# Neighbourhood attention: the turning of the weights is multiplied by a diagonal of reciprocal sums

## The reference

```python
s_loc = jnp.einsum("bqhd,biqjhd->bhqij", q_r, k_win).astype(jnp.float32) * scale
s_loc = s_loc + bias.astype(jnp.float32)
s_ctx = jnp.einsum("bqhd,bchd->bhqc", q_r, kc).astype(jnp.float32) * scale
s = jnp.concatenate([s_loc.reshape(B, H, GRID_W, n_loc), s_ctx], axis=-1)
p = jax.nn.softmax(s, axis=-1).astype(v.dtype)
p_loc = p[..., :n_loc].reshape(B, H, GRID_W, kh, NA_KW)
return (jnp.einsum("bhqij,biqjhd->bqhd", p_loc, v_win)
        + jnp.einsum("bhqc,bchd->bqhd", p[..., n_loc:], vc))
```

## Time and profile before

| what | us |
|---|---|
| median of three executions (lowest, highest) | 3058.83 (3057.3, 3061.13) |
| the profiled execution | 3055.73 |
| its span, first to last instruction | 3053.9 |
| TensorE busy with matmuls in it | 2975.5 |
| VectorE busy | 2074.0 |
| ScalarE busy | 1412.6 |
| GpSimd busy | 241.1 |
| all turning matmuls of the attention (line 2296), within 1978 to 2104 us | 9.66 |

### The profile page before, as it was taken

How to read it: one execution, slowest core, us unless ns; L and a number is a source line. 1 busy time by engine, 2 the same in 40 slices (tenths; PEclk the granted TensorE clock), 3 DMA queues, 4 the chain that set the end, 5 groups by cost and what they waited for, 6 DMA issues and landing times.

```text
span 3053.9 us, 52430 instructions
## 1 busy us (share of the span) xinstructions
PE 2975.5 (97%) x21994; PEld 2632.0 (86%) x21994; DVE 2074.0 (68%) x2869; ACT 1412.6 (46%) x1977; POOL 241.1 (8%) x201
## 2 busy tenths in 40 slices
PE   8999999999999999999999999999989999999998
PEld 7899988887888888888888899888878888888887
DVE  6486864645656787888888985555677666666666
ACT  5343542534444563544445454444336445444453
POOL 1100321110100200000000310010010000000002
PEclk9999999999999999999999999999999999999999
DMA  7555566766645669888888877755345565665664
GB/s 250 166 167 156 158 222 206 225 196 227 209 138 159 214 198 280 274 277 277 273 279 277 271 234 225 221 151 170 109 131 162 183 187 178 202 187 184 180 186 132
DMA packets 527580, 619.94 MB, mean 203 GB/s; under 512 B 19450, under 2 KB 443541, under 8 KB 525984
## 3 DMA queue, kind: packets, MB, share of 16 engines
q1 hardware_dynamic: 518672, 586.31, 62.2%
q0 software_dynamic: 3344, 23.78, 2.2%
q10 hardware_dynamic: 5328, 6.49, 0.6%
HBM read 608.12 MB, written 8.39 MB: 202 GB/s over the span
## 4 chain that ended last, share of the span: by engine, by line
PE 90%; DVE 5%; issue 3%; ACT 1%; DMA 0%; POOL 0%; ACTq 0%; POOLq 0%; DVEq 0%; SPq 0%
PE psum L605 37%; PE psum L606 19%; PE psum L574 6%; PE psum L576 6%; PE psum L577 6%; PE psum L639 2%; PE psum L641 2%; PE psum L642 2%; DVE wlo L531 1%; PE psum L1851 1%; PE psum L706 1%; DVE cacc L1118 1%; PE psum L2563 1%; PE psum L2082 0%; PE psum L2304 0%
## 5 line engine op out<-in xcount | busy, mean ns | idle before, releaser
L524 ACT ACTIVATE whi<-wraw 128x1024 fp32r<-128x1024 f32 (+1 forms) x948 | 978.6, 1034 | 1001.2 <-PE psum L606 692.7
L531 DVE TENSOR_TENSOR wlo<-wraw,whi 128x1024 fp32r<-128x1024 f32 (+1 forms) x948 | 1151.2, 1230 | 244.6 <-ACT whi L524 244.1
L605 PE MATMUL psum<-g,whi 128*128 128x512 f32 x2816 | 996.1, 396 | 11.0 <-DVE g L2603 4.1
L605 PE MATMUL psum<-h,whi 128*128 128x512 f32 x2240 | 790.7, 395 | 2.3 <-DVE wlo L531 1.3
L606 PE MATMUL psum<-g,wlo 128*128 128x256 f32 x2816 | 787.0, 279 | 0.0
L605 PEld LDWEIGHTS psum<-g,whi 128*128 128x128 f32 x2816 | 529.0, 188 | 139.9 <-issue 8.4
L606 PE MATMUL psum<-h,wlo 128*128 128x256 f32 x2240 | 634.1, 283 | 0.0
L606 PEld LDWEIGHTS psum<-g,wlo 128*128 128x128 f32 x2816 | 529.2, 188 | 0.5
L605 PEld LDWEIGHTS psum<-h,whi 128*128 128x128 f32 x2240 | 421.4, 188 | 100.3 <-DVE wlo L531 1.6
L606 PEld LDWEIGHTS psum<-h,wlo 128*128 128x128 f32 x2240 | 421.9, 188 | 0.1
L574 PE MATMUL psum<-h,whi 128*128 128x256 f32 x1040 | 304.0, 292 | 22.0 <-DVE h L958 13.7
(11 more groups left out here) (488 smaller groups left out, 3191.3 us busy)
## 6 DMA issues: line engine op xcount, KB each, us to landing
wraw<-in_ffn_w SPq DMA_DIRECT2D x256, 512.0 KB, 4.9
wraw<-in_w_in SPq DMA_DIRECT2D x204, 512.0 KB, 3.7
wraw<-in_ada_w SPq DMA_DIRECT2D x192, 512.0 KB, 4.2
wraw<-in_ffn_w_up SPq DMA_DIRECT2D x160, 512.0 KB, 3.6
wraw<-in_w_out SPq DMA_DIRECT2D x64, 512.0 KB, 3.7
wraw<-in_ffn_w_down SPq DMA_DIRECT2D x64, 512.0 KB, 4.5
wraw<-in_xattn_wk SPq DMA_DIRECT2D x32, 512.0 KB, 4.6
wraw<-in_xattn_wv SPq DMA_DIRECT2D x32, 512.0 KB, 4.9
```

Of the source, the lines that this page charges most:

```text
L524: e.activation(high(i), raw(i), ACT.Copy).then_inc(*hi.up(i))
L531: e.tensor_tensor(low(i), raw(i), high(i).bitcast(F32), SUB).then_inc(*lo.up(i))
L605: e.matmul(both_of(g, j), w_hi[:, kk, s:s + 128], X[:, k, :], start=k == 0, stop=False, skip_group_check=True)
```

## The change

The reciprocal of each unit's sums is no longer multiplied into the 128x512 buffer. VectorE multiplies the 128x128 identity by it and writes the diagonal matrix to a new tile, `DG`, with two buffers. The turning takes this diagonal as its moving side, and is a plain matmul, `e.matmul`, in place of `e.transpose`. The result in bank 5 is the same: block transposed, each query's column scaled. For units from 2 on, VectorE waits before it writes `DG` until the turning of two units earlier has read the same buffer.

```diff
@@ -342,6 +342,7 @@
         TMX = new("tmx", [P, 4, T])
+        DG = new("dg", [P, 2, P])
@@ -2293,7 +2294,8 @@
                         for k in range(4):
-                            x = e.transpose(PSUM[:, 5, 128 * k:128 * k + 128], weights_of(u)[:, 128 * k:128 * k + 128], ident)
+                            x = e.matmul(PSUM[:, 5, 128 * k:128 * k + 128], weights_of(u)[:, 128 * k:128 * k + 128], DG[:, u % 2, :], start=True,
+                                         stop=True)
                         x.then_inc(*nat.p.up(("pt", u)))
@@ -2321,11 +2323,13 @@
         def na_share_v(e, u):
-            p, s = weights_of(u), SM6[:, u % 8, :]
+            s = SM6[:, u % 8, :]
             e.wait_ge(*nat.a.at("e", u))
             e.reciprocal(s[:, 3:4], s[:, 2:3]).then_inc(*nat.v.up())
             e.wait_ge(*nat.v.now())
-            e.tensor_scalar(p, p, s[:, 3:4], None, MUL).then_inc(*nat.v.up(("p", u)))
+            if u > 1:
+                e.wait_ge(*nat.p.at("pt", u - 2))
+            e.tensor_scalar(DG[:, u % 2, :], ident, s[:, 3:4], None, MUL).then_inc(*nat.v.up(("p", u)))
```

## The result

Nine executions of the changed kernel took 3061.9 to 3070.5 us, with a median of 3065.3; nine of the kernel before had a median of 3058.0. The ratio on record is 1.0027, with a 95% interval of 1.0019 to 1.0035; the quotient of the two medians is 1.0024. So the changed kernel is slower, by 7.3 us between the medians. The forecast was 7.6 us more and 3066.4.

The account below looks back on a forecast made before the run. TensorE was taken to bound the attention's stretch. 7.4 us for second passes plus 0.2 for idle starts, with VectorE's saving hidden, made 3058.8 + 7.6 = 3066.4 us; the forecast's own range was 3065 to 3068, 8 in 10 3062 to 3070.

Parts of the forecast that it names:

- What bounds the stretch: Attention, 1978 to 2104 us: TensorE, busy 122.3 of 126 us, sets the end; anything added to its stream moves it.
- The second pass: Turning on TensorE: a plain float32 matmul makes two passes per call, 0.46 us more a unit, 7.4 us in 16 units.
- The value of 0.112 taken from line 1281: Turning on TensorE: time of one float32 pass in us, read from line 1281's same-shaped matmuls; eight make 0.90 us.
- The small term: Three units whose turning begins on an idle TensorE after the copy: 3 x 0.07 = 0.2 us more.
- VectorE's saving: VectorE's 16 multiplications, 128x128 in place of 128x512: 3.2 us saved, none of it on the path.
- The cover of unit 0: Attention: unit 0's division ends 6.8 us before its turning releases the chain, the narrowest of the 16.
- The 288 ns worked out for the diagonal: VectorE: time taken for one 128x128 multiplication, in place of 486 ns for 128x512.
- The added wait: VectorE before writing `DG`: of 3.46 us between turning and reciprocal, 3.0 us are left, so the wait costs nothing.
- Nothing absorbs it: TensorE's waits keep their length and later work moves whole; wrong if what follows the stretch changes by over 3 us.
- A plain matmul at a transpose's cost: Rival at the 64 turning calls: eight passes fit into 0.44 us, nothing is added, 3055.6 to 3058.8 us; chance 6%.
- One at four transposes: Rival at the turning: a plain float32 matmul costs four transposes, 1.32 us more a unit, 21 us, 3080; chance 2%.
- The slow clock: Rival, later in the block: stretches at clock 0.50 may go, saving 4.4 us, sum 3.2 us, 3062.0; chance 14%.

Follow-up runs that it names:

- Experiment 5: Kernel before, with VectorE multiplying each unit's 128x512 buffer by one four times more ahead of the division: ratio 0.9997, 3057.4 us beside 3058.6.
- experiment 6: Changed kernel with one buffer for the diagonal, so VectorE waits for the turning of the unit before: ratio 1.0019, 3064.7 us beside 3058.6 for the kernel before.
- experiment 2: Kernel before, with each unit's four transposes issued twice: ratio 1.0024, 3065.6 us beside 3057.6.
- experiment 8: Changed kernel with turning, scores and product with the values all in the rounded format: ratio 0.9927, 3037.7 us beside 3058.6 for the kernel before.
- experiment 1: Kernel before, with the turning as a plain float32 matmul against the identity and the division left on the 128x512 buffer: ratio 1.0021, 3065.2 us beside 3057.6.
- experiment 3: Changed kernel with the turning as a transpose against the identity again; the diagonal is written but unread: ratio 0.9998, 3057.2 us beside 3057.6 for the kernel before.
- experiment 7: Changed kernel with each block turned by two matmuls with stationary sides of 64 columns: one execution at 3069.1 us.
- experiment 4: Changed kernel with the diagonal and the exponentials written in the rounded format: ratio 0.9996, 3056.4 us beside 3057.6 for the kernel before.

## Why the prediction was right

- *What bounds the stretch.* Right. Experiment 5 gives VectorE 30.1 us more and experiment 6 makes it stand for 54.7, and the end doesn't move; experiments 2 and 8 add and take passes of TensorE, and the end moves by +6.94 and -20.00 us, as the passes say.
- *The second pass, 16 x 0.46 = 7.4 us.* Right: 128 records, 0.89 us for eight, 7.40 us in the stretch, and 7.35 in experiment 1 with nothing else changed. The value of 0.112 taken from line 1281 holds (0.89 / 8 = 0.111); experiment 2 puts the passes' count at 6.94 of it.
- *The small term, 0.2 us for groups on an idle engine.* Too large. With the term the stretch should have grown by 7.6, and it grew by 7.40. The group that starts after the wait stands with 1.13 us in the chain where the transposes' had 0.63 (in the chain as in the earlier trace rows), 0.05 more than the 0.45 that other groups gained (0.89 against 0.44), so 0.15 us in three units, and by the chain's figures the other groups gained 0.01 less than the 0.46 taken. The term was mis-sized by line 1281, whose first step is 0.10 over the others. A turning group on an idle engine lasts 1.13 us in order of time and the others 1.05, so that the plain matmul loses 0.08 there and not 0.10.
- *VectorE's saving, 3.2 us, hidden.* Right in both: experiment 3 has 3.14 us less and no gain. The cover of unit 0, given as 6.8 us, is 6.6 by the start of its turning; that reading decides nothing. The 288 ns worked out for the diagonal were 287 in the median. In the changed kernel itself the saving was 1.2 us (71.42 to 70.24), since more of the short instructions met GpSimd (last section); it cost nothing, being hidden.
- *The added wait.* Right, with no wait in the trace. Only the 3.0 us left of 3.46 is wrong. The changed kernel still has the 3.46, from the end of unit 6's turning to unit 8's reciprocal:

```profile
2041.90 1.05 PE L2297 MATMUL psum<-dg,tmx 128*128 128x128 f32 x8
...
2046.41 0.15 DVE L2328 RECIPROCAL sm<-sm 128x1 f32<-128x1 f32 x1
```

The reciprocal waits for work that hangs on TensorE itself, so it moves when the turning gets longer. Experiment 6 shows that even a wait that stands costs nothing here. The reason given ahead of that run, two chunks' low halves in store, is read from the order of the programs; the run shows only that TensorE's waits stay at 2.3 and 1.4 us.
- *Nothing absorbs it.* Right: TensorE's waits stay at 3.7 us. What lies after the stretch was 2.08 us shorter in the profile, less than the 3 set as a bound, and the medians differ by 7.3.
- *The rivals.* A plain matmul at a transpose's cost is off by experiment 1. One at four transposes would have made it 21 us more. By experiments 1 and 2 the two differ by 132.94 - 132.53 = 0.41 us at an equal number of passes, so nearly all of the mode's gain at 128 columns is the halved count, 0.89 / 0.44 = 2.0. The rule behind that rival, in the table of terms of the Trainium skill's TensorE: Matmul & The Clock Gate, is that the transposing mode is 4x faster for FP32; this trace doesn't agree, with 2.0. The slow clock did move, as the other rival had it, and in part its way: in the profiled execution of the changed kernel nothing stands at 0.50 where the first stretch of the earlier trace rows would be, but one near 2300 us lasts 6.8 us in place of 3.4. No gain of 4.4 us came of it, and it differs from execution to execution.

## What to carry to other kernels

Count the passes of a matmul before moving work to it: where a float32 transpose becomes a float32 matmul, its records double, and where TensorE sets the end each of them is on the path, here 64 x 0.112 us. An engine's saving is worth what the stretch's last wait says, and a dose in the other direction (experiment 5, ten times the saving, spent) shows at once whether it is worth anything. Where executions scatter by several us, cut the span at the same two instructions in both traces: the 7.4 us stood out to 0.05 us in each profile, while the times needed nine runs and more to show them.

## What the runs showed of the hardware

*The slow clock comes and goes between executions.* Up to the first score matmul the profiled executions took 1977.0 (experiment 1) to 1984.7 us (experiment 2), with the same instructions in all (in experiment 8 some write another format). In the changed kernel the granted clock was 0.50, 1.2 GHz, in stretches where it was 1.00 before, and the reverse. After:

```profile
368.70:372.00 3.30, 3.30 (x18) 3.30 (x17) 3.30 (x8) 0.24 (x1) 0.37 (x1) 0.50 0.00 1
...
2217.20:2223.90 6.70, 6.70 (x34) 4.49 (x32) 4.94 (x5) 0.00 (x0) 1.27 (x1) 1.00 0.02 9
```

Before, the first of these stood at the full clock and the second, of the earlier trace rows, at 0.50:

```profile
368.70:372.00 3.30, 3.30 (x31) 3.30 (x30) 3.30 (x7) 0.63 (x1) 1.13 (x1) 1.00 0.16 57
```

TensorE gets 18 matmuls through the first in place of 31. Ahead of the attention this goes far to account for the differences. The times of the ten profiles broadly follow the time that each spent at 0.50, added up from the traces' granted clock:

| at 0.50 ahead of the attention, us | profiles | first score matmul at, us |
|---|---|---|
| 13.7 | before, experiments 1 and 5 | 1977.0 to 1978.7 |
| 17.1 | experiments 7 and 8 | 1979.2 and 1980.0 |
| 20.5 | after, experiments 3 and 6 | 1979.1 to 1981.0 |
| 23.9 | experiment 4 | 1984.2 |
| 27.3 | experiment 2 | 1984.7 |

The 6.8 us between before and after can cost 3.4 at most, since the clock is halved, and the measured difference is 1.88. Behind the attention the clock doesn't suffice. Leaving out the very end, where TensorE has next to nothing to do, before was at 0.50 for 13.7 us and after for 10.2, which can give 1.7 us of the 2.08; and experiments 1 and 3, at 0.50 for 17.1 us, took 948.4 and 949.5 there, less than the 949.6 of before. What the rest is stays open. No such stretch fell into the attention in any of the profiles.

*VectorE's multiplication is held while GpSimd adds.* Three of the 16 diagonals took 1.1 us in place of 0.29. Each began while GpSimd's addition of bias and mask ran and ended about 0.1 us after it; one that began ahead of it, at 2031.80, took its usual time:

```profile
1999.96 1.29 POOL L2267 TENSOR_TENSOR bi<-bi,ms 128x512 f32<-128x512 f32 x1 [2.47 <-DMA bi<-in_bias]
2000.03 0.16 DVE L2328 RECIPROCAL sm<-sm 128x1 f32<-128x1 f32 x1
2000.22 1.12 DVE L2332 TENSOR_SCALAR dg<-mats,sm 128x128 f32<-128x128 f32 x1
...
2031.80 0.29 DVE L2332 TENSOR_SCALAR dg<-mats,sm 128x128 f32<-128x128 f32 x1
2031.95 1.26 POOL L2267 TENSOR_TENSOR bi<-bi,ms 128x512 f32<-128x512 f32 x1 [3.89 <-DMA bi<-in_bias]
```

The reciprocal that began inside the same addition took its usual 0.16 us, so not every instruction of VectorE is held. It also explains the 589 ns mean against 486 in the earlier trace rows: one of the eight took 1.31 us. No experiment took GpSimd's addition away, so that it holds VectorE is read from the times alone.
